# Block-wise gates-to-queries stages in the first pass of a hybrid decoder step, with the first block's experts begun in the second of them, and whole weight tiles per transfer

## What is computed

```python
proj = x @ w_in                                   # z, xbc, dt, u, v, gates
y_a = ssd_branch(z, xbc, dt, ...)                 # conv, silu, chunked scan over 128 tokens, gated RMS norm
y_b = chunk_sgu_branch(uv, ...)                   # gelu, layer norm of v, 128x128 spatial mixing, times u
g_a, g_b = split(sigmoid(gates))
merged = g_a * (y_a @ w_branch_a) + g_b * (y_b @ w_branch_b)
h = layer_norm(alpha * x + merged @ w_out)
q = h @ w_q                                       # 8 heads, two halves of 128
top_s, top_i = top_k(q_half @ sub_keys.T, 16)     # per head and half
best_s, best_c = top_k(all 16x16 sums, 16)        # 16 experts per head: 128 per token
act = gelu(h . u_tab[expert])                     # 128 rows of u per token
out = layer_norm(alpha * h + sum_k softmax(best_s)_k * act_k * v_tab[expert_k])
```

## Time and profile before

| | |
|---|---|
| median of 3 runs | 5205.01 us (5204.82 to 5212.57) |
| profiled execution, its span | 5205.6 us, 48526 instructions |
| pass 0: scan, v and u, back | to 705, to 959, to 1820 us |
| pass 1: scan, v and u, back | to 2621, to 2914, to 3812 us |
| tail | 3812 to 5205 us |
| moved by DMA | 1674.5 MB, of them 1133.7 MB on GpSimd's queue (q0) and 536.5 MB on SyncE's (q1) |
| PE busy, DVE busy, POOL busy | 87%, 54%, 43% |

### The profile page before, as it was taken

The page is one execution under the profiler, slowest core; times in us unless marked ns, Lnnn a source line. Parts: engine busy times, 40 slices in busy tenths (PEclk is TensorE's granted clock), DMA queues, the critical chain, the costliest instruction groups (busy, mean ns, idle before and its releaser), DMA issues. The chain is left out here.

```text
span 5205.6 us, 48526 instructions
## 1 busy us (share of the span) xinstructions
PE 4523.2 (87%) x18494; PEld 3370.4 (65%) x18494; DVE 2803.0 (54%) x3713; ACT 858.0 (16%) x1941; POOL 2236.7 (43%) x1647
## 2 busy tenths in 40 slices
PE   8999999999999897897789798999857777887776
PEld 6888878888887686776677687787733332332222
DVE  4565622000002678898866665666876655364445
ACT  2333311100000133333301110000111111110000
POOL 3676640000000345454533523455578875364442
PEclk9999999999999998998899899999978899899999
DMA  6766664445554499999999899999999999999998
GB/s 204 228 212 218 199 194 130 139 147 165 165 187 123 125 390 397 417 417 408 403 364 394 338 416 398 397 417 417 376 383 422 421 422 419 382 400 422 421 421 368
DMA packets 331808, 1674.51 MB, mean 322 GB/s; under 512 B 47201, under 2 KB 62113, under 8 KB 195873
## 3 DMA queue, kind: packets, MB, share of 16 engines
q0 software_dynamic: 160640, 1133.71, 53.3%
q1 hardware_dynamic: 165768, 536.51, 30.0%
q10 hardware_dynamic: 5168, 1.19, 0.1%
HBM read 1633.31 MB, written 37.89 MB: 321 GB/s over the span
## 5 line engine op out<-in xcount | busy, mean ns | idle before, releaser
L584 PE MATMUL psum<-rows_a,w_ring 128*128 128x264 f32 x6656 | 1499.2, 387 | 13.7 <-PEq L539 8.9
L584 PEld LDWEIGHTS psum<-rows_a,w_ring 128*128 128x128 f32 x6656 | 1263.3, 191 | 233.9 <-issue 19.0
L584 PE MATMUL psum<-x_and_spare,w_ring 128*128 128x256 f32 x5632 | 1263.6, 385 | 81.9 <-PEq L539 69.1
L584 PEld LDWEIGHTS psum<-x_and_spare,w_ring 128*128 128x128 f32 x5632 | 1080.3, 193 | 251.6 <-issue 92.8
L392 POOL DMA_INDIRECT rows_a<-in_peer_u,expert x384 | 723.7, 1885 | 922.7 <-DVE rows_a L447 857.6
L447 DVE SCALAR_TENSOR_TENSOR rows_a<-rows_a,h_tokens 128x2048 f32<-128x2048 f32 x388 | 889.0, 2293 | 366.4 <-DMA rows_a<-in_peer_u,expert 305.5
L392 POOL DMA_INDIRECT rows_a<-in_peer_v,expert x382 | 506.5, 1326 | 375.6 <-PE psum L491 167.6
L491 PE MATMUL psum<-rows_b,diags 128*128 128x512 f32 x1008 | 483.6, 629 | 193.9 <-ACT diags L481 147.7
L491 PE MATMUL psum<-rows_a,diags 128*128 128x512 f32 x1008 | 488.8, 635 | 149.5 <-ACT diags L481 101.7
L491 PEld LDWEIGHTS psum<-rows_b,diags 128*128 128x128 f32 x1008 | 194.0, 200 | 482.5 <-issue 296.9
L491 PEld LDWEIGHTS psum<-rows_a,diags 128*128 128x128 f32 x1008 | 195.9, 202 | 441.7 <-issue 301.1
(11 more groups left out here) (372 smaller groups left out, 3385.7 us busy)
## 6 DMA issues: line engine op xcount, KB each, us to landing
w_ring<-in_w_tiles SPq DMA_DIRECT2D x896, 512.0 KB
rows_a<-in_state_ssm POOLq DMA_DIRECT2D x32, 512.0 KB, 5.7
out_ssm_sample<-rows_a POOLq DMA_DIRECT2D x32, 512.0 KB, 5.5
rows_a<-acum_rows_dram SPq DMA_DIRECT2D x16, 512.0 KB, 5.0
rows_a<-smp_bc_dram POOLq DMA_DIRECT2D x8, 1024.0 KB, 8.3
acts_by_token<-late SPq DMA_DIRECT2D x16, 512.0 KB, 6.7
branch_b<-acum_rows_dram SPq DMA_DIRECT2D x16, 512.0 KB, 7.5
rows_a<-in_xT SPq DMA_DIRECT2D x3, 2048.0 KB, 18.1
```

What stands on the lines that cost most here:

```text
L584: last = pe.matmul(o, w[:, k * P:(k + 1) * P], x[:, k, :], start=start and k == 0, stop=stop and k == KB - 1)
```

## The change

- Pass 0 keeps its `ssd` and `sgu` for 264 tokens at once (`Front`). Its `back` is done twice (`Back`): first a for block 0 (n = 128), then b for block 1 and the samples (n = 136). Both read all 112 tiles of the stage, so 112 tiles more are loaded. Pass 1 is one `Front` and one `Back` c, of 256 tokens, as before.
- The selection of block 0 is done for heads 0 and 1 in a's stage q, for heads 2 to 7 in b's gates. That of block 1 is done for heads 0 and 1 in b's stage q, for heads 2 to 7 in pass 1's scan, one in each of groups 0 to 5. Each head is chosen for one block at a time. Scores wait in a tile of their own (`kept`).
- 32 of the 256 slots are worked off in b; the rest is dealt anew over pass 1.
- Each weight tile is one transfer of 1 MiB (8 KiB per partition): a slot of the ring is loaded again when its whole tile is used, and the matmuls wait for the whole tile.
- The activations of the scan and the x columns are stored and loaded by block, the state of the scan lies in another buffer.

```diff
-PASS_CHUNKS = ((0, 2), (2, 2))
+FRONT_CHUNKS = ((0, 2), (2, 2))
+BACK_CHUNKS = ((0, 1), (1, 1), (2, 2))
+BACKS_OF = ((0, 1), (2,))
+RING = 3
+for _backs in BACKS_OF:
+    STREAM += ORDER[:O_GATE]
+    WHOLE += [True] * O_GATE
+    for _b in _backs:
+        STREAM += ORDER[O_GATE:]
+        WHOLE += [True] * (N_TILES - O_GATE)
...
-STEPS_B = (13, 20, 16, 32, 15, 32, 16, 3, 18)
+STEPS_B = (8, 4, 8, 4, 4, 4)
+STEPS_F = (10, 15, 18)
+STEPS_C = (30, 15, 29, 15, 3, 19)
...
+            if WHOLE[q]:
+                if q >= RING:
+                    sp.wait_ge(self.w_used, q - RING + 1)
+                sp.dma_start(slot, tile).then_inc(self.w_in[q % RING][0], 16)
...
+        heads = [(1, p) for p in range(EARLY, PH)] if ex else []
+        choose_at = {(i, 2): i for i in range(len(heads))}
+        share_at = {(i, 6): i for i in range(len(heads))}
...
+                    if (g, c) in choose_at:
+                        i = choose_at[g, c]
+                        act.wait_ge(ranked, i + 1)
+                        if i >= 2:
+                            act.wait_ge(self.gate_done, PH + EARLY + i - 1)
+                        top.exps(o, act, i).then_inc(chosen_exp, 1)
...
+        late = [(0, p) for p in range(EARLY, PH)] if ps.smp else []
+        late_at = {2 + 5 * i: i for i in range(len(late))}
+        late_share = {c + 3: i for c, i in late_at.items()}
...
+                if ps.smp:
+                    x_wide = self.backs[2].n
+                    sp.dma_start(self.shared[:, 0:KB * x_wide].rearrange("p (k t) -> p k t", k=KB),
+                                 a["xT"][:, :, self.backs[2].first:TP]).then_inc(self.x_next, 16)
```

More of the change, by code:

```diff
@@ L610, in plan, with back @@
         tiles = lambda name, count, first=0: [(name, n) for n in range(first, count)]
[L611 to L621, removed]
+        def back(name, gate, wb, wa, mix, ln, q):
+            put(name, tiles("gate", 2 * FT), gate)
+            put(name, tiles("wb", FT), wb)
+            put(name, tiles("wa", FT), wa)
+            put(name, tiles("out", FT), mix)
+            put(name, tiles("ln", 2), ln)
+            put(name, tiles("q", FT), q)
+        back("b", *STEPS_B)
+        scan, v, u = STEPS_F
+        for g in range(G):
+            put("f1", [("ssd", g, c) for c in range(9)], scan)
+        put("f1", tiles("v", FT), v)
+        put("f1", tiles("u", FT), u)
+        back("c", *STEPS_C)
         assert s == SLOTS
@@ L704, in first_pass @@
             late = flat(rows_a)[:, KB * ps.n:KB * (ps.n + TP - ps.np)].rearrange("p (k t) -> p k t", k=KB)
+            yb_two = sb("branch_b_two", [P, KB * P + 2 * two.n])[:]
+            own = self.region(flat(rows_a)[:, 2 * every:])
+            own = [own(KB, one.n) for _ in range(3)]
             self.make = self.tables(xs, late)
             self.smp = Samples(self, cut, sb)
-            self.one_pass(ps, xs, spare, yb, m_acts, None)
-    def later_pass(self, ps, ex):
+            kept = self.kept[:]
@@ new lines, in first_pass @@
+            by_tile = lambda x, n: x[:, 0:KB * n].rearrange("p (k t) -> p k t", k=KB)
+            gated = [by_tile(yb, ps.n)[:, :, 0:one.n], by_tile(yb_two, two.n)]
+            self.stage(lambda st: self.ssd(st, ps, xs, spare, yb, m_acts, None))
+            self.stage(lambda st: self.sgu(st, ps, xs, spare, yb, m_acts, gated, None))
+            xs_two = by_tile(flat(self.htok[:, CH - 2:CH, :]), two.n)
+            self.stage(lambda st: self.back(st, one, xs[:, :, 0:one.n], own, gated[0], yb, self.late[:], spare, kept,
+                                            xs_two, None))
@@ new lines, in later_pass, with stage @@
+            gated = [self.region(yb)(KB, ps.n)]
+            kept = self.region(self.late[:])(2 * PH, ps.n)
+            self.stage(lambda st: self.ssd(st, ps, xs, spare, yb, m_acts, ex))
+            self.stage(lambda st: self.sgu(st, ps, xs, spare, yb, m_acts, gated, ex))
+            self.stage(lambda st: self.back(st, three, xs, (xs, gated[0], xs), gated[0], yb, m_acts, spare, kept,
+                                            None, ex))
+    def stage(self, build):
+        with ExitStack() as st:
+            build(st)
+        self.clear_sems()
@@ L1988, in _ @@
                 dve.wait_ge(ln["summed"], 1)
-                for m in range(FT if pick else 0):
+                for m in range(FT):
                     p = m // 3 - 1
```

421 lines of the change are left out of this document (231 added, 190 removed).

## The result

The changed kernel takes **5254.79 us** (median of 4 runs) against 5206.99 us of the kernel before in the same session: ratio **1.009**, 95% interval 1.0075 to 1.0104. It is slower by 0.9%, where 5157 us, 0.9% less, was forecast. Its profiled span is 5257.3 us, 51.7 us above that of before.

The account below looks back on a forecast made before the run. TensorE alone bounds pass 0's back; from 1820 us DMA is nearly full, with VectorE and TensorE's chain also near their limits in pass 1's scan. Terms +61 - 64 - 15 - 25 - 5 = -48 from 5205.6 gave 5157 us, range 5085 to 5260.

Parts of the forecast that it names:

- term 5: Weight transfers of whole tiles: nearly even where DMA is not alone the bound, -5 us (-26 to +15).
- Term 1, b: Second half of the split back, pass 0: DMA ends last, 490 us (460 to 560); a and b together +61 us.
- b above 540 us: Sign listed as showing the forecast wrong; stage b was expected at 475 to 510 us with DMA share near 1.
- weights come late in b: Rival, chance 0.08: gathers and weights share the engines in b, which takes 590 us; 5257 us in all.
- Pass 0's scan, "nothing": Pass 0's scan, v and u do the same arithmetic; extra stores and products lie under matmuls: no change.
- Term 1, a: First half of the split back, pass 0: 110 ns per 128-column matmul, 432 us; a and b together +61 us.
- Term 2: Pass 1's scan, 80 slots for 104 and six choices: half of TensorE's waits go, 737 us, -64 us.
- The rival of the choices: Rival, chance 0.13: choices take the slots' place in pass 1's scan, which stays near 785 us; 5205 us in all.
- Term 3: Pass 1's v and u, 33 slots for 36, 6.3 MB less at 384 GB/s: -15 us (-5 to -20).
- term 4: The last back, 111 slots for 116, 10.5 MB less at about 397 GB/s: -25 us (-10 to -30).
- DMA alone is the bound from b on: Rival, chance 0.22: from b's start only bytes count, 1484 MB at 401 GB/s; 5092 us in all.
- The narrow matmul pays for its load: Rival, chance 0.12: 128-column matmuls in a and b slow to 150 ns a pair, 5382 us; at 191 ns, 5676 us.

Follow-up runs that it names:

- x3: The changed kernel with no slots in b, pass 1 having all 256 slots by the old numbers: 5328.5 us, ratio 1.0224.
- x1: The changed kernel with every weight tile loaded in two halves again, nothing else changed: 5230.45 us, ratio 1.0033 against the kernel before.
- y1: The changed kernel with tiles in halves in all of pass 0 and whole tiles in pass 1: 5198.89 us, ratio 0.9978 against the kernel before.
- x2: The kernel before with every weight tile in one transfer, nothing else changed: 5212.17 us, ratio 1.0006.
- x6: The changed kernel with GpSimd's sample-state updates in pass 0's scan done for one sample of eight: 5215.44 us (one run).
- x4: The kernel before with the scan's state in the changed kernel's buffer, and the wait that goes with it: 5214.22 us, ratio 1.0011.
- z1: The kernel before with whole tiles in pass 1 alone, without the split: 5196.69 us, ratio 0.9975.
- z5: y1 with 24 slots in b in place of 32, and 11 per group of pass 1's scan in place of 10: 5222.18 us, ratio 1.0028.
- z3: y1 with 9 slots per group in pass 1's scan in place of 10, and 8 more in v and u: 5217.91 us, ratio 1.0016.
- y2: y1 with 48 slots in b for 32, and 8 per group in pass 1's scan for 10: 5283.94 us, ratio 1.0128.
- z4: y1 with 6 slots moved from the last back to pass 1's v and u: 5215.03 us, ratio 1.001.

## Why the prediction was wrong

The measured span is 100 us above the forecast's 5157 us. The forecast was too low for b by 68 us, for the start and pass 0's scan by 32, for pass 1's v and u by 16 and for a by 12. It was too high for the last back by 23 and for pass 1's scan by 12. The rest is term 5's -5 and small differences. The time lies in the prediction's widest range (5085 to 5260 us), but near its upper end, where only the case of late weights had put it.

*Term 1, b: the step that failed.* "195 MB at 401 GB/s = 487 us. DMA ends last": the bytes were right (195.9 MB), the time was 558. The prediction took the larger of two floors, 450 us of TensorE and 487 us of DMA, and nothing for their meeting. The first was 33 us too low: without slots b already takes 483 us (x3). And from there the slots are not free up to a bound of DMA, but add a price each: 2.3 us for each of 32 in whole tiles, 2.0 to 2.8 for the last 8 of 32 in halves, 4.1 to 4.5 past 32. And b as a whole moved 351 GB/s at a share of 0.91, not the 401 counted on; with halves it is 366 GB/s at 0.96. The sign that the prediction itself named, b above 540 us, came. Of its rivals it is "weights come late in b", given 0.08: 50.5 us of waiting for weights are there, with halves 29.6 (x1) and 34.3 (y1). That this rival's 5257 us is the measured span is luck: its b was 590 us, 32 too long, and pass 0's scan, for which it had nothing, made up for it.

Why a slot costs what it does is argued and not shown. Weights come in one queue, gathers in another, and over b's fortieths the rate swings between 220 and 423 GB/s; the likely reading is that a tile which comes late costs time that a later lull does not give back, with only three slots in the ring. No run had a deeper ring or other gather sizes.

*Pass 0's scan, "nothing": failed.* It is +30 us. The prediction read arithmetic and not timing: VectorE and GpSimd already ran into one another there before, in two groups of seven, and now do in all seven. x1 and x2 give it to the whole tiles, x6 to the collision, x4 clears the state.

*Term 1, a: 432 forecast, 444.5 measured.* The price of the narrow matmul was right (110 ns taken, 112 measured). Of the 12 us, 6 are whole tiles (x1).

*Term 2: right in kind, -76 for -64.* x3 splits it: choices +50, 24 slots fewer -126. The waits were halved as forecast (107.6 to 50.5 us over the two largest), and DMA moves 371 GB/s at a share of 0.92 (364 GB/s forecast). One reading behind it was wrong: VectorE's 667.68 us were not "nearly all" slots, which have 237.7 + 230.2 = 468 us of them; the sum did not use it. The rival of the choices had a true mechanism, 9 us in each group with one, but the slots won back more. A slot fewer brought 5.5 us down to 10 per group, less than 2 from 10 to 9, and at 8 the scan is longer again: 11, 10, 9 and 8 per group give 769, 725, 711 and 742 us.

*Term 3: failed, +1 for -15.* The 384 GB/s of the earlier trace rows was read as a bound. With halves v and u take 292.4 and 292.9 us with 36 slots and 294.1 with 33; with whole tiles 296 to 298 us with 36 and 293 to 294 with 33. So three slots bring nothing, or some 3 us that whole tiles cost. TensorE has 251 to 255 us there and a barrier (19.1 us of waiting at L567), and DMA's share falls to 0.89. With 39 and 41 slots it takes 16 and 30 us more, 12 and 13 of them in a wait for ScalarE.

*Terms 4 and 5.* The last back gained 48: 17 to 22 by whole tiles (x2, x1), and 26 by the 5 slots fewer (x1: 869.8 for 895.7), the -25 of term 4. Term 5 had the range for pass 1's gain (up to -26), but set it for the kernel as a whole; pass 0 takes 54 us for it (25 + 6 + 23).

Summed, in halves and whole tiles where each is better (y1): a + b +108, scan -76, last back -48, pass 0's scan +4, v and u of both passes +2, the tail -5: -16 us by the profiled spans, some 12 by the ratio of the runs (the +4 and the -5 are within what one execution varies). 17 of it is the whole tiles' part of the last back, which z1 has without the split; what is left for the split cannot be told from nothing. *DMA alone is the bound from b on* is refuted: it needed 401 GB/s from b to the end, and b, the scan, v and u moved 351, 371 and 361. *The narrow matmul pays for its load* is refuted by 112 ns. Open are why 8 slots per group are worse than 9 and 10, and which transfer shifts VectorE against GpSimd. On the first there is a trace: the wait for ScalarE at L1220 is 35.3, 25.8, 1.9, 7.7 and 30.3 us with 13, 11, 10, 9 and 8 slots per group (x3, z5, the changed kernel, z3, y2). It does not follow how many slots there are, which leaves where they stand between the convolutions, but no run moved them alone.

## What to carry to other kernels

A stage with two loads, here a stream of weights and gathers, did not cost the larger of its floors: measure its length with one load away, and add a price for each piece of the other, which here was 2.3 us for the first 32 slots and over 4 for the next. Bytes bought in one stage to save bytes in another are to be priced at both ends, and a byte saved is worth something only down to the next floor of its stage (z4: 6 slots fewer in the last back, 2 us). Where two engines lock one another out, a change that alters no instruction of a stage can still lengthen it; so test a change of transfer size by stage, and keep it where it gains. That DMA is nearly full does not foretell the sign: whole tiles gained in the last back and lost in b. And before a large change is judged, time the smallest part of it alone on the kernel before (z1).

## What was not expected of the hardware

- Three VectorE instructions of 128x256 took 4.55 us in place of 1.55 beside GpSimd's TENSOR_TENSORs of 128x1024; the product L1362 took 3220 ns on average, and 1410 with these units short. Pass 0's scan loses by it even in the kernel before: it takes 672.7 us, and 657.3 with whole tiles and seven eighths of the samples' work left out.
- A matmul of 128 columns with new weights each time: 112 ns over thousands of pairs, 116 with 136 columns. Weight loads, each recorded with a mean of 195 ns in a, add at most 4 ns to the 108 that 128 columns are by the 223 ns of 264.
- The same choice of transfer size had both signs in one kernel: -17 to -22 us in the last back with DMA at a share of 0.98, +18 to +25 in pass 0's scan at 0.58, where bandwidth is no limit at all, and +23 in b at 0.91.
- TensorE's granted clock turned 18 us of added waits in pass 0's scan into 30 us: 11 more are the same matmuls at a mean clock of 0.97 in place of 0.99.
